# A two-layer decoder kernel: the next pair's w1 requests go ahead of this pair's w3 and w2 requests

## The reference

```python
def block_mlp(args):
    xb, e = args
    hdn = jax.nn.silu(xb @ w1[e]) * (xb @ w3[e])
    return hdn @ w2[e]
...
out = jnp.zeros((n_tok + 1, d), y.dtype).at[row_tok].add(y * row_w[:, None].astype(y.dtype))
```

## Time and profile before

| what | before |
|---|---|
| median of 3 runs | 2094.64 us (2092.26 to 2095.2) |
| the profiled execution's own time | 2092.71 us |
| its span | 2090.9 us |
| PE busy | 1896.9 us (91%) |
| DVE busy | 753.3 us (36%) |
| ACT busy | 503.7 us (24%) |
| POOL busy | 104.4 us (5%) |
| moved by DMA | 478.11 MB, mean 229 GB/s |

### The profile page before, as it was taken

How to read it: one execution, slowest core, us unless ns; L and a number is a source line. 1 busy time by engine, 2 the same in 40 slices (tenths; PEclk the granted TensorE clock), 3 DMA queues, 4 the chain that set the end, 5 groups by cost and what they waited for, 6 DMA issues and landing times. The chain is left out here.

```text
span 2090.9 us, 22829 instructions
## 1 busy us (share of the span) xinstructions
PE 1896.9 (91%) x8452; PEld 937.7 (45%) x8452; DVE 753.3 (36%) x1449; ACT 503.7 (24%) x785; POOL 104.4 (5%) x84
## 2 busy tenths in 40 slices
PE   7899999999699999999979899979599999999978
PEld 5565555666433333333334475466433333333333
DVE  2444444442423433343331111164424333343331
ACT  3233333332111111111130423542111111111130
POOL 0111111110000000000000000000000000000000
PEclk8999999999799999999989999989799999999999
DMA  6111111020589999999971212111299999999931
GB/s 226 41 40 41 41 41 40 0 81 1 206 346 420 421 422 421 421 421 421 421 290 40 81 41 88 40 41 41 104 378 421 421 421 421 421 422 422 421 118 41
DMA packets 77071, 478.11 MB, mean 229 GB/s; under 512 B 6352, under 2 KB 6736, under 8 KB 26576
## 3 DMA queue, kind: packets, MB, share of 16 engines
q1 hardware_dynamic: 72400, 460.46, 53.9%
q0 software_dynamic: 4608, 16.78, 2.0%
HBM read 470.93 MB, written 6.29 MB: 228 GB/s over the span
## 5 line engine op out<-in xcount | busy, mean ns | idle before, releaser
L1322 PE MATMUL bank<-ring,xT 128*64 128x512 f32 x2048 | 467.6, 602 | 48.4 <-DMA ring<-in_w 47.3
L1322 PEld LDWEIGHTS bank<-ring,xT 128*64 128x64 f32 x2048 | 138.5, 137 | 327.1 <-issue 238.3
L1296 DVE TENSOR_TENSOR H<-H,bank 128x512 f32<-128x512 f32 x256 | 171.1, 688 | 261.0 <-PE bank L1309 260.5
L375 PE MATMUL bank<-ring,ring 128*128 128x512 f32 x512 | 250.4, 601 | 8.9 <-ACT ring L682 8.9
L1346 PE MATMUL bank<-ring,hT 128*64 128x512 f32 x1024 | 226.8, 596 | 0.5 <-ACT hT L1362 0.5
L1309 PE MATMUL bank<-yp,Sb 128*128 128x512 bf16 x768 | 189.4, 383 | 6.9 <-issue 6.4
L1309 PEld LDWEIGHTS bank<-yp,Sb 128*128 128x128 bf16 x768 | 67.4, 98 | 147.0 <-issue 83.3
L1346 PEld LDWEIGHTS bank<-ring,hT 128*64 128x64 f32 x1024 | 70.7, 137 | 133.0 <-issue 128.0
L843 PE MATMUL bank<-ring,ring 128*128 128x512 f32 x288 | 126.4, 593 | 0.2
L1283 DVE TENSOR_TENSOR y<-y,yp 128x512 f32<-128x512 f32 x64 | 44.3, 692 | 197.1 <-ACT yp L1371 197.1
L375 PEld LDWEIGHTS bank<-ring,ring 128*128 128x128 f32 x512 | 86.4, 193 | 59.7 <-issue 49.5
(11 more groups left out here) (237 smaller groups left out, 2070.8 us busy)
## 6 DMA issues: line engine op xcount, KB each, us to landing
ring<-in_w SPq DMA_DIRECT2D x192, 2048.0 KB, 26.2
ring<-in_w_heads SPq DMA_DIRECT2D x8, 2048.0 KB, 8.2
ring<-in_w_ple_gate SPq DMA_DIRECT2D x4, 2048.0 KB, 31.3
ring<-in_w_kv SPq DMA_DIRECT2D x3, 2048.0 KB, 14.7
ring<-in_b_w_q SPq DMA_DIRECT2D x3, 2048.0 KB, 8.2
ring<-in_a_w_out SPq DMA_DIRECT2D x2, 2048.0 KB, 13.9
rows<-ring SPq DMA_DIRECT2D x8, 512.0 KB, 10.6
H<-in_x SPq DMA_DIRECT2D x4, 512.0 KB, 4.9
```

The source lines that it names most:

```text
L375: m = pe.matmul(bank[j % 2][:, :], w[:, c, j, :], k.xnT[:, c, :], start=(c == 0), stop=(c == DC - 1))
L1296: dve.tensor_tensor(out, out, k.bank[6 + j % 2][:, :], ALU.add).then_inc(s.added, 1)
L1322: last = pe.matmul(out[e * SLOTS:(e + 1) * SLOTS, :], k.xT[:, at, e * SLOTS:(e + 1) * SLOTS], w[:, e, c, :], start=(at == 0), stop=(at == ...
```

## The change

`load_expert_pair` takes a new argument, `slots`, and issues only those of the six pieces that it names. SP's block in `experts` uses it to issue slots 0 and 1 of the next pair ahead of slots 2 to 5 of the pair before. The waits before each piece, the buffers and the pieces themselves are the same. (`expert_slot` looks at `odd` only for slots 0 and 1.)

```diff
-def load_expert_pair(k, layer, pair, load, odd=False):
+def load_expert_pair(k, layer, pair, load, odd=False, slots=range(RING)):
...
             slot = 2 * m + half
+            if slot not in slots:
+                continue
             load(slot, expert_slot(k, slot, odd).rearrange("p (e x) -> p e x", e=2),
...
             sp.wait_ge(k.rows_stored, 16 * NT)
             sp.wait_ge(s.xg, 16)
-            load_expert_pair(k, layer, 1, load_of(1, True), odd=True)
+            load_expert_pair(k, layer, 1, load_of(1, True), odd=True, slots=(0, 1))
             with sp.Fori(1, PAIRS // 2) as j:
-                load_expert_pair(k, layer, 2 * j, load_of(2 * j, False))
-                load_expert_pair(k, layer, 2 * j + 1, load_of(2 * j + 1, True), odd=True)
+                load_expert_pair(k, layer, 2 * j, load_of(2 * j, False), slots=(0, 1))
+                load_expert_pair(k, layer, 2 * j - 1, load_of(2 * j - 1, True), slots=(2, 3, 4, 5))
+                load_expert_pair(k, layer, 2 * j + 1, load_of(2 * j + 1, True), odd=True, slots=(0, 1))
+                load_expert_pair(k, layer, 2 * j, load_of(2 * j, False), slots=(2, 3, 4, 5))
+            load_expert_pair(k, layer, PAIRS - 1, load_of(PAIRS - 1, True), slots=(2, 3, 4, 5))
```

## The result

| | before | after |
|---|---|---|
| median | 2094.50 us (9 runs) | 2099.44 us (9 runs, 2096.11 to 2100.96) |
| ratio, 95% interval | | 1.0023 [1.0013, 1.0033], so +4.8 us, 2.7 to 6.9 |
| span of the profiled execution | 2090.9 us | 2094.3 us |
| expert stage, layer 0 | 476.69 us | 479.93 us |
| expert stage, layer 1 | 477.21 us | 479.67 us |

What follows compares the result with a forecast made beforehand. The prediction took the weight transfers at 421 GB/s to bound the expert stages; +2.99 us (layer 0) and +2.52 (layer 1) made +5.5, so 2098.2 for the profiled execution and, 1.9 above, a median of 2100.1 us, range 2095 to 2106.

Steps and rivals of the forecast that it cites:

- What bounds the stage: Expert stages: TensorE leads at first, then weight transfers set 31.11 us a pair against its own 28.34, 2.77 us of waiting.
- The gap at the start: Start of each expert stage: earlier requests keep the queue from running dry, gaining 5.20 us in layer 0, 5.64 in layer 1.
- The shift by two pieces at the end: End of each stage: w3b of pair 14 lands 9.96 us later; waits of 1.77 and 1.80 us behind it vanish.
- The waits: Expert stages: TensorE waits for weights before w3a and w3b alone, from pair 3 or 4, none behind w3b of 14.
- Sum and total: Whole kernel: +2.99 us in layer 0 and +2.52 in layer 1, together +5.5, giving 2100.1 us.
- The last byte as the only bound: Rival, stage end: a fixed time behind the landing of pair 15's w2b; -10.8 us, 2083.8 us; chance 0.07.
- the gap stays open: Rival, stage start: late requests or a straggling transfer, so the shift is paid in full; +16.3 us, 2111.0; chance 0.05.
- absorbed by the gather: Rival, pair 15: its gather of token rows comes behind w3b of 14, 1.25 us less per layer; +3.0, 2097.6; chance 0.08.
- The clock did not fall: Rival, before the last pair: gathered waits lower TensorE's clock, 1.5 us per layer; together +8.5, 2103.1 us; chance 0.10.

Runs made afterwards that it cites:

- back_at_14: Changed kernel, but slots 2 to 5 of pair 14 go ahead of slots 0 and 1 of pair 15 again; 2094.17 us, ratio 1.0002.
- middle_only: Kernel before, but slots 0 and 1 of pairs 7 to 10 go ahead of slots 2 to 5 of pairs 6 to 9; 2094.91 us, ratio 1.0000.
- late_start: Changed kernel without its first exchange: slots 0 and 1 of pair 2 stay behind slots 2 to 5 of pair 1; 2110.26 us, ratio 1.0084.
- one_ahead: Changed kernel, but from pair 3 on only slot 0 goes ahead of the pair before, slot 1 follows it; 2091.32 us, ratio 0.9985.
- first_only: Kernel before with the first exchange alone: slots 0 and 1 of pair 2 ahead of slots 2 to 5 of pair 1; 2086.89 us, ratio 0.9961.
- last_only: Kernel before with the last exchange alone: slots 0 and 1 of pair 15 ahead of slots 2 to 5 of pair 14; 2116.39 us, ratio 1.0108.
- back_at_9: Changed kernel's order up to pair 8, order of the kernel before from pair 9 on; 2085.23 us, ratio 0.9963; in more rounds 2086.93 us, ratio 0.9965.
- back_at_12: Changed kernel's order up to pair 11, order of the kernel before from pair 12 on; 2086.86 us, ratio 0.9963.

## Why the prediction was right

*What bounds the stage.* Right. The queue at 421 GB/s sets 31.11 us per pair, TensorE alone 28.34; back_at_14's 28.35 us from w3b to w3b shows the second, the return of the waits after four pairs in middle_only shows their difference, since 9.96 us at 2.77 a pair are 3.6 pairs.

*The gap at the start.* Right in kind and nearly in size. The requests stood at 587.65 and 591.08 where I had 587 and 590.5. I had taken 5.20 and 5.64 us from the slices' rates and supposed all of it closed. The changed kernel moved w3b of pair 14 by 1020.33 - 1015.02 = 5.31 us, of which 0.16 is a later start (579.05 against 578.89), so 9.96 - 5.15 = 4.81 us were won; in layer 1, 5.12 less 0.71 of later start, 5.55. late_start gives 4.90 and 5.24 for the same. In layer 0, 590 to 598 runs at 407 GB/s, not 421, which is 0.27 us, most of the difference.

*The shift by two pieces at the end.* Right, and the heart of it. late_start isolates it: +8.14 and +7.70 where 9.96 less 1.77 and 1.80 are 8.2. One piece instead of two (one_ahead) makes it -4.59 in the stages instead of +5.70, 10.3 us less, where two transfers' time is 9.96.

*The waits.* Right. After the change they stand before w3a and w3b alone and begin at w3b of pair 3 (678.34), and behind w3b of 14 none is left, 41.75 us against the 41.90 I had summed.

*Sum and total.* +5.5 predicted, +5.7 in the stages, +4.9 in the medians; 2100.1 against 2099.44. Part of that closeness is luck. The other stages differ by 1 to 3 us between executions: the profiled one of first_only enters its first expert stage 3.4 us later than that of the kernel before, and between the two expert stages the profile has 457.68 us before and 454.99 after, although nothing there was changed. Of these 2.69 us, 1.19 are the spread of layer 0, which ran at a lower clock before (0.62; 7.54 us) and not after (6.35).

*The rivals.* The last byte as the only bound is refuted by back_at_14, last_only and one_ahead. A piece that the closed gap brings earlier does bound back_at_9, though the last one waited for is w1b of pair 15 and not the last byte, and there my price for it, -10.8, stands in the stages as -11.1; back_at_12, with -10.9, lies where the two bounds meet. That the gap stays open is refuted by the slices. Nothing of the shift was absorbed by the gather: for pair 15 GpSimd issues it at 1008.99, 11.3 us before w3b of pair 14 starts, and before the change it was 1003.62, 11.4 us ahead. The clock did not fall in the changed kernel, whose waits reach 1.7 us in layer 0 (2.0 in layer 1, over a granted 1.00). The Trainium skill's account of a wait for a transfer that throws the clock to half ("TensorE: Matmul & The Clock Gate", "HAM oscillation — how this bites in real kernels") did not decide here, but last_only shows it at work.

## What to carry to other kernels

When the queue of transfers is the bound, ask of a new request order not only whether the queue stays full but which piece the computing engine waits for last, and how much of its own work lies behind that piece: a piece moved ahead costs every piece that it passes one transfer's time, here 4.98 us. That price is invisible in the steady stretch and is paid at the end of the loop, unless the order is turned back early enough, here three pairs of 2.77 us for a price of 8.2 (the shift of 9.96 less the 1.8 of waits that vanish). So let an order that fills a gap at the start end before the loop does; measured, that made 5 us of loss into 7 us of gain. And where the engine comes to wait in one long piece, look at its clock behind the wait.

## What the runs showed of the hardware that was not expected

Whether TensorE's clock falls behind a wait was not settled by the length of the wait alone. Waits of 1.7 us (the changed kernel), 2.0 us (its layer 1) and 2.40 us (middle_only, w3b of pair 14, 1016.43) were followed by a granted 1.00. The four waits of 11.14 to 11.17 us (last_only and middle_only, both layers) were followed by the lower level, and w3a took 6.30 to 6.55 us for 3.65. In between lies one of late_start, where a wait of 2.81 us was followed by 3.4 us at a granted 0.51 and the group took 5.35 us; later waits of that kernel absorbed it.

```profile
677.30 5.35 PE L1324 MATMUL bank<-ring,xT 128*64 128x512 f32 x16 [2.81 <-DMA ring<-in_w]
```

```profile
677.80:681.20 3.40, 3.40 (x11) 0.98 (x9) 0.00 (x0) 0.00 (x0) 0.00 (x0) 0.51 1.03 425
```

One stop of the same length stands in every trace, twice: after the last pair of either layer TensorE is idle for 3.20 us while the results are scaled and split, and then spreads. Before and after the change, layer 0:

```profile
1061.88 7.54 PE L1309 MATMUL bank<-yp,Sb 128*128 128x512 bf16 x24 [3.20 <-issue]
```

```profile
1065.28 3.06 PE L1311 MATMUL bank<-yp,Sb 128*128 128x512 bf16 x12 [3.20 <-issue]
1068.78 2.85 PE L1311 MATMUL bank<-yp,Sb 128*128 128x512 bf16 x11 [0.44 <-DVE H L1298]
```

In the eleven traces of this case (back_at_9 has two) the clock fell behind 17 of these 22 stops, and the spread then took 7.5 to 7.7 us; behind the other five it stayed at 1.00 and the spread took 6.3 to 6.4. The five are layer 1 before, both layers of the changed kernel, and layer 1 of back_at_14 and first_only. So the same stop costs 1.2 us in one execution and nothing in another, which is a part of why the other stages scatter. What decides between the two was not found.

Gathering a pair's 2.77 us of waiting into one place, as late_start does in that one pair, was thus followed once by a lower clock. The changed kernel, whose longest wait is 2.0 us, lost none.
